# A hybrid layer on one core: S5 blocks in smaller TensorE tiles, a new order in both attentions, and the order of the last banks

## What is computed

```python
hn = rms_norm(h, norm_mix); proj = hn @ w_in          # u, q, k, v of 512 each
y_ssm = s5_mixer(u, ...)                              # 32 groups, 64 complex states each
y_att = moba_attention(q, k, v, rel_bias)             # 8 heads of 64, blocks of 256
mixed = concat([rms_norm(y_ssm, g1), rms_norm(y_att, g2)])
h = h + mixed @ w_out
h = h + memory_cross_attention(rms_norm(h, g3), rms_norm(mem, g4), x_wq, x_wkv, x_wo, x_qn, x_kn)
h = h + conv_ffn(rms_norm(h, g5), ffn_w_up, conv_w, conv_b, ffn_w_down)
```

## Time and profile before

| | |
|---|---|
| median of three runs | 713.04 us (709.05 to 714.66) |
| the profiled execution | 710.0 us |
| its span, first to last instruction | 708.4 us |
| PE busy | 694.4 us (98% of the span) |
| PEld busy | 576.2 us (81%) |
| VectorE, ScalarE, GpSimd busy | 412.8, 316.3, 142.6 us |
| granted TensorE clock | 1.000 of full |
| DMA | 73.94 MB, mean 104 GB/s |

### The profile page before, as it was taken

How to read it: one execution, slowest core, us unless ns; L and a number is a source line. 1 busy time by engine, 2 the same in 40 slices (tenths; PEclk the granted TensorE clock), 3 DMA queues, 4 the chain that set the end, 5 groups by cost and what they waited for, 6 DMA issues and landing times.

```text
span 708.4 us, 10868 instructions
## 1 busy us (share of the span) xinstructions
PE 694.4 (98%) x3913; PEld 576.2 (81%) x3913; DVE 412.8 (58%) x697; ACT 316.3 (45%) x535; POOL 142.6 (20%) x139
## 2 busy tenths in 40 slices
PE   7999999999999999989999999999999999999998
PEld 7978888886777888878998888888888887888886
DVE  4998967737665556556965555555555563333333
ACT  5737344467744635663554433343333432322220
POOL 4899985033031111240100000000000000000000
PEclk9999999999999999999999999999999999999999
DMA  8748443277310033030313323233133132231303
GB/s 249 222 116 142 138 117 108 67 218 247 139 60 2 29 121 119 1 119 1 120 60 120 104 73 118 75 103 118 60 118 108 69 118 98 80 118 67 111 1 118
DMA packets 62998, 73.94 MB, mean 104 GB/s; under 512 B 20873, under 2 KB 47796, under 8 KB 62836
## 3 DMA queue, kind: packets, MB, share of 16 engines
q1 hardware_dynamic: 59172, 66.12, 29.5%
q10 hardware_dynamic: 3792, 7.36, 3.3%
HBM read 68.08 MB, written 5.78 MB: 104 GB/s over the span
## 4 chain that ended last, share of the span: by engine, by line
PE 88%; POOL 4%; DVE 3%; ACT 2%; DMA 1%; issue 1%; SPq 0%; ACTq 0%; DVEq 0%; POOLq 0%
PE pb L514 25%; PE pb L516 25%; PE pb L515 25%; PE pb L1797 9%; PE pb L1800 4%; POOL F L692 2%; DMA raw<-in_w_in 1%; ACT F L900 1%; DVE F L1282 1%; ACT xs L900 0%; DVE wring L500 0%; ACT L900 0%; POOL F L805 0%; POOL F L808 0%; POOL rt L692 0%
## 5 line engine op out<-in xcount | busy, mean ns | idle before, releaser
L514 PE MATMUL pb<-xs,wring 128*128 128x512 f32 (+1 forms) x448 | 165.2, 369 | 1.2 <-POOL xs L832 0.7
L516 PE MATMUL pb<-xs,wring 128*128 128x512 f32 (+1 forms) x448 | 164.1, 366 | 0.0
L515 PE MATMUL pb<-xs,wring 128*128 128x512 f32 (+1 forms) x448 | 164.1, 366 | 0.0
L497 DVE TENSOR_TENSOR wring<-raw,wring 128x1024 fp32r<-128x1024 f32 x95 | 122.5, 1292 | 71.5 <-ACT wring L486 71.3
L486 ACT ACTIVATE wring<-raw 128x1024 fp32r<-128x1024 f32 x100 | 105.0, 1053 | 87.3 <-PE pb L516 75.0
L1288 DVE SCALAR_TENSOR_TENSOR F<-pb,ccol,F 128x511 f32<-128x511 f32 x88 | 66.0, 750 | 103.4 <-ACT F L900 97.5
L514 PE MATMUL pb<-wring,bs 128*128 128x512 f32 x240 | 96.1, 400 | 1.3 <-DVE bs L1288 0.9
L514 PEld LDWEIGHTS pb<-xs,wring 128*128 128x128 f32 x448 | 84.5, 189 | 15.7 <-POOL xs L832 1.2
L516 PEld LDWEIGHTS pb<-xs,wring 128*128 128x128 f32 x448 | 84.5, 189 | 13.7
L515 PEld LDWEIGHTS pb<-xs,wring 128*128 128x128 f32 x448 | 84.5, 189 | 13.5
L516 PE MATMUL pb<-wring,bs 128*128 128x512 f32 x240 | 93.6, 390 | 0.0
(11 more groups left out here) (147 smaller groups left out, 788.4 us busy)
## 6 DMA issues: line engine op xcount, KB each, us to landing
raw<-in_ffn_w_up SPq DMA_DIRECT2D x22, 1024.0 KB, 5.1
raw<-in_ffn_w_down SPq DMA_DIRECT2D x11, 1024.0 KB, 4.8
F<-in_x SPq DMA_DIRECT2D x8, 512.0 KB, 5.6
raw<-in_w_in ACTq DMA_DIRECT2D x4, 1024.0 KB, 5.6
raw<-in_w_out SPq DMA_DIRECT2D x4, 1024.0 KB, 5.0
raw<-in_w_in SPq DMA_DIRECT2D x3, 1024.0 KB, 6.0
raw<-in_x_wkv ACTq DMA_DIRECT2D x3, 1024.0 KB, 6.0
raw<-in_x_wq SPq DMA_DIRECT2D x2, 1024.0 KB, 6.2
```

Source lines behind the costliest of these rows:

```text
L497: ins = nc.vector.tensor_tensor(w_unit(u, 1), raw_unit(u), w_unit(u, 0).bitcast(f32), ALU.subtract)
L514: nc.tensor.matmul(ps, lh, rh, start=first, stop=False)
L515: nc.tensor.matmul(ps, lh, rl_, start=False, stop=False)
L516: return nc.tensor.matmul(ps, ll, rh, start=False, stop=last)
```

## The change

**S5 on TensorE.** In `kernels_in` the four pairs a go to four groups of 32 partitions of the bank and of array columns (before: to four column ranges of one bank at partition 0), and the loop over the parts is outside the loop over a. ScalarE copies each pair out by itself: eight operations of 16 by 128 in place of two of 16 by 512. In `outputs` each matmul is cut in two halves of 64 weight columns, c = 0 and 1, which go to the lower and upper 64 partitions of the same bank.

**Order around the own attention.** The write of the last quarter of S5's output is issued before chunk 12 (the gate's weight) is loaded; `skip_in(3)` and `gelu(3)` stand one step earlier, at 4; unit 26 is split at step 9 (before 8), unit 27 at 11 (before 9); the second tile of the memory's values is copied at 9 (before 8); the low part of unit 29 is taken at step 18 behind `ya_scale(1)` (before at 17, ahead of it).

**Memory attention.** One piece of the query projection less goes ahead of the loop, and each step from 0 to 15 has one piece: steps 0 to 6 the query projection, 7 to 15 the output projection. Transposes, high and low parts of the outputs are one step earlier, `qx_rows(2)` and `(3)`, their sums and roots one or two later, the residual of tile 0 is at 10 and 12, half of that of tile 1 at 14. All four low parts of `x_wo` on GpSimd stand ahead of the power of query tile 3 (before: two of the four). `QXT_BANK`, `XO_BANK` and `W_BANK` give other banks.

**Down projection.** The banks are taken in the order 4, 5, 6, 7, 0, 1, 2, 3, and the outputs leave in that order.

```diff
-XO_AT = [4, 5, 6, 8]
+XO_AT = [5, 6, 7, 8]
-SPLIT_AT = {0: 22, 1: 23, 2: 24, 4: 25, 8: 26, 9: 27, 13: 28, 16: 29, 29: 30, 31: 31}
+SPLIT_AT = {0: 22, 1: 23, 2: 24, 4: 25, 9: 26, 11: 27, 13: 28, 16: 29, 29: 30, 31: 31}
...
-        XO_BANK, W_BANK = (0, 2, 1, 7), (0, 1, 2, 0, 3, 1, 2, 3)
+        D_ORDER = (4, 5, 6, 7, 0, 1, 2, 3)
+        QXT_BANK, XO_BANK, W_BANK = (0, 1, 2, 0), (1, 0, 1, 7), (2, 1, 2, 0, 2, 1, 3, 2)
...
             load_chunk(sync, 11)
+            y_write(NQ - 1)
             load_chunk(sync, 12)
             y_back(NQ - 1)
...
                 if EV[i][0] == "qx2":
                     pool.wait_ge(lo_done, U_XO)
-                    output_low(0)
-                    output_low(1)
-                if EV[i][0] == "qx3":
-                    output_low(2)
-                    output_low(3)
+                    for n in range(4):
+                        output_low(n)
...
                 for b, n in enumerate("ab"):
-                    evac(f"k{n}{q}", kt[0:CG].rearrange("p (a b) n -> p a b n", b=2)[:, :, b, :],
-                         lambda p: p[0:CG, :].rearrange("p (a n) -> p a n", a=QP))
+                    p = read(act, f"k{n}{q}")
+                    for a in range(QP):
+                        last = A_(kt[0:CG, 2 * a + b, :], p[32 * a:32 * a + CG, 0:128], ACT.Copy)
+                    drained(last, f"k{n}{q}")
...
-                if s == 5:
+                if s == 4:
                     gelu(3)
-                if s in (7, 8):
-                    mem_rows("mv", xv, s - 7)
+                if s in (7, 9):
+                    mem_rows("mv", xv, s // 9)
...
-                if s - 1 in SPLIT_AT:
+                if s - 1 in SPLIT_AT and SPLIT_AT[s - 1] != U_OUT + 3:
                     split_lo(dve, SPLIT_AT[s - 1])
+                if s == 2 * H + 2:
+                    split_lo(dve, U_OUT + 3)
...
-                if s in (3, 7):
-                    qx_event(2 + s // 4)
-                if s in (2, 4, 8):
+                if s in (4, 8):
+                    qx_event(1 + s // 4)
+                if s in (2, 6, 10):
                     root(f"qx{1 + s // 4}", qr_ready)
...
-                for a in range(QP):
-                    at = slice(a * (L + 1) * CG, a * (L + 1) * CG + L * CG)
-                    for part in range(2):
+                for part in range(2):
+                    for a in range(QP):
+                        at = slice(a * (L + 1) * CG, a * (L + 1) * CG + L * CG)
                         for b in range(2):
                             rows = slice(b * NS, (b + 1) * NS)
-                            last = mm(p[b][0:CG, a * 128:(a + 1) * 128], bb[rows, part, q * QP + a, :],
+                            last = mm(p[b][32 * a:32 * a + CG, 0:128], bb[rows, part, q * QP + a, :],
                                       ca[rows, q % 2, part, at], part == 0, part == 1)
...
-                    mm(p[b][:, a * NC:(a + 1) * NC], toep[:, g, :], ub[:, q * QG + g, :], True, False)
-                at = slice((a * (L + 1) + 1) * CG, (a + 1) * (L + 1) * CG)
+                    for c in range(2):
+                        half = slice(c * 64, c * 64 + 64)
+                        mm(p[b][half, a * NC:(a + 1) * NC], toep[:, g, half], ub[:, q * QG + g, :], True, False)
+                at = (a * (L + 1) + 1) * CG
                 for part in range(2):
-                    for b in range(2):
-                        rows = slice(b * NS, (b + 1) * NS)
-                        last = mm(p[b][:, a * NC + 1:(a + 1) * NC], ca[rows, q % 2, part, at],
-                                  zb[rows, part, a, 0:NC - 1], False, part == 1)
+                    for c in range(2):
+                        half = slice(c * 64, c * 64 + 64)
+                        for b in range(2):
+                            rows = slice(b * NS, (b + 1) * NS)
+                            last = mm(p[b][half, a * NC + 1:(a + 1) * NC],
+                                      ca[rows, q % 2, part, at + c * 64:at + c * 64 + 64],
+                                      zb[rows, part, a, 0:NC - 1], False, part == 1)
...
-                if s < 2 * XH - 2:
-                    if s == 2:
+                if s < 2 * XH - 1:
+                    if s == 3:
                         x2_ready(3)
-                    xq_piece((s + 2) // XH + 2, (s + 2) % XH)
-                elif s >= 2 * XH:
-                    if s % XH == 0:
-                        after_drain(pe, f"xo{s // XH - 2}")
-                    xo_piece(s // XH - 2, s % XH)
+                    xq_piece((s + 1) // XH + 2, (s + 1) % XH)
+                else:
+                    if (s + 1) % XH == 0:
+                        after_drain(pe, f"xo{(s + 1) // XH - 2}")
+                    xo_piece((s + 1) // XH - 2, (s + 1) % XH)
...
-                for b in range(8):
+                for b in D_ORDER:
```

63 lines of the change are left out of this document (32 added, 31 removed).

## The result

| | before | after |
|---|---|---|
| median of the runs | 713.27 us (709.05 to 714.66) | 704.87 us (704.0 to 705.36) |
| profiled execution | 710.0 us, span 708.4 | 705.13 us, span 703.5 |

The ratio is 0.9917 (0.9888 to 0.9947). A second timing of the changed kernel on another chip gave 703.15 us against 709.73, 0.9903 (0.9888 to 0.9917). The medians are thus 6.6 to 8.4 us apart, the two profiled executions 4.9 us; 9.8 had been forecast for the latter. (The recorded ratio is not the quotient of the two medians, which is 0.988 in the first timing.)

A forecast was written before the change was run, and what follows sets the result against it. PE, busy 98% of the span, was taken as the bound. S5 6.3, own attention 2.0, memory attention 0.8 and down projection 0.7 summed to 9.8 us, from 710.0 to 700.2; median put at 702, forecast range 698 to 705.

The forecast's parts named there:

- rival (4): Tiles work, but early gelu(3) and late power cost what the other edits save: 703, median 705; chance 0.14.
- rival (2): S5's tiles pay in part: matmul starts become the limit, output pieces gain nothing; 704, median 706; chance 0.17.
- S5's tiles, the work: PE in S5: 0.20 us less for each of 16 output pieces, 1.2 less for each of four quarters' kernels.
- Rivals (1) to (3): S5's tiles: (1) only two at once, 0.12; (2) part of it, 0.17; (3) slower, column tiles exclude each other, 0.07.
- S5's tiles, the gain: S5 gives 6.3 us (0 to 7.5), with 1.5 arriving past VectorE's scan and 4.8 behind it.
- Behind it no such close meeting is left: S5 after VectorE's scan: savings of quarters 1 to 3 arrive in full, 4.8 us.
- The three other quarters have 2 us or more: S5's Toeplitz tables after the first quarter: 2 us or more of room before PE would wait for them.
- The own attention (a): Gate's first piece: earlier result write and gelu(3) shorten its wait for GpSimd; net 0.6 us gained, after 0.3 for probabilities.
- (b): Own attention step 8: PE's 1.13 us wait for ScalarE's copy of the probabilities shrinks, 0.7 gained.
- (c): Own attention step 18: PE's 0.90 us wait for `ya_scale(1)` shrinks as it goes ahead of unit 29's low part, 0.7 gained.
- Memory attention: Projection pieces cover PE's 1.8 us idle at steps 6 to 8; 0.8 gained (-0.3 to 1.8), VectorE setting the up projection's start.
- Down projection: First down unit's wait at bank 3 is covered by taking that bank last; 0.7 us gained.

The follow-up runs named there:

- S5 alone: Kernel before with S5's small array tiles (kernels_in, outputs, ScalarE's copies), all orders as before: median 708.56 against 709.70 us, ratio 0.9984, profiled 707.6.
- the orders as a whole: Changed kernel with S5's matmuls and copies as before, leaving the attention and down projection orders: median 706.45 against 709.70 us, ratio 0.9953.
- all in order: Changed kernel with reordered loads and splits, gelu(2) behind two probabilities, gelu(3) and skip_in(3) at step 5, chunk 12 before last write: 702.93 against 710.19 us, 0.9884.
- kernels' tiles alone: Kernel before with only the eight tiles for S5's kernels and ScalarE's eight copies: median 711.58 against 711.34 us, ratio 0.9996, profiled 707.7.
- gelu alone back: Changed kernel with gelu(3) and skip_in(3) back at step 5, last write still ahead of chunk 12: median 702.48 against 709.73 us, ratio 0.9907.
- second version of the bias: Changed kernel with chunk 10, then bias, ahead of quarter 2's read; gelu(0), gelu(1) and low parts earlier, gelu(2), skip_in(2) later: 704.58 against 711.34 us, 0.9883.

## Why the prediction was right in its time, and where its steps failed

The time, 704.87 against 702, is in the range, but that is partly luck. It lies at the upper edge of the forecast's 698 to 705 and nearest to rival (4), *the orders don't pay*, with 705; a median alone doesn't choose between them and rival (2) with 706. The sum behind it, 9.8 us, was twice what the traces show (4.9, of which 0.8 is start-up). Two steps failed, and a term is missing: the sum has nothing for the clock, which took 1.7 us in the profiled execution and up to 3.4 in others.

- **S5's tiles, the work**: right. Piece 1.09 us (forecast 1.07 to 1.17), kernels' block 0.58 (0.6), together 8.4 us of PE's work (3.2 + 4.8 = 8.0). Rivals (1) to (3) fall. The rule of the Trainium skill (TensorE: Matmul & The Clock Gate, Part 3) that a weight load overlaps a running matmul only where the row group differs would let column tiles gain nothing, as the prediction reads it; these rows disagree: the column tiles save the time in full.
- **S5's tiles, the gain**: wrong. The scan's wait was foreseen (over 1 us; 1.51 measured, though not in every execution). "Behind it no such close meeting is left" and "The three other quarters have 2 us or more" failed: I had looked for room at the next engine and not at the transfers. The last table had 2 us only as long as chunk 10's load came after it; with PE early, ScalarE issued that load before the table's last DMA. And behind it the loads, the bias and the first probabilities were a chain: in the seven traces with all tiles and the bias where it was, PE waits 1.5 to 2.9 us between 140 and 158, wherever the waits sit. S5 alone gave 1.1 us in the median and 2.4 in the profiled execution, not 6.3.
- **The own attention (a)**: wrong in sign. Forecast 0.6 gained; the gate's 0.73 went and 2.75 came. "units 24 and 25 are split later; they are needed at step 8 only" looked at PE's need, but ScalarE takes its steps in order, and its copies for step 5 stand behind the split. The early gelu(3) with its two table loads was priced at 0.3 and cost 0.99 even without S5. To that extent rival (4)'s mechanism came true, though the orders as a whole paid 3.3 us. The prediction named this among what would show it wrong: a wait for probabilities at step 6 of over 1 us; it was 1.73.
- **(b) and (c)**: right, 0.72 and 0.70 against 0.7 each.
- **Memory attention**: 0.9 against 0.8, with the up projection's start set by VectorE, now with a wait of 1.00 at it. No wait at bank 2. **Down projection**: 0.8 against 0.7.
- The rest is start-up and clock: PE was 0.8 us earlier at 43 us already, and the kernel before's median was 3.3 above its profiled execution in the first timing, 0.3 below it in the second, where all its executions had the full clock.

Not tried: all in order with gelu(3) at step 4. Open: what makes the clock fall in one execution and not in the next, on which the spread of the kernels' tiles alone (7.6 us) hangs.

## What to carry to other kernels

When an edit makes the busiest engine early, follow every queue at the place where it will arrive: an order between two queues that held by a microsecond is no order. A wait of an in-order engine is paid by what stands behind it there, whoever needs the awaited thing; and where removing one wait leaves the time as it was, look for where it came back. Compare when the next transfer's user starts in each trace, but ask in each what issued the transfer: equal times can have different causes, as chunk 12's had. And take the granted clock of each execution along: here it moved the time by as much as the edits did.

## What the runs showed of the hardware

- 24 records of an output piece, 8 on 128x64 tiles and 16 on 64x64, take 0.77 us; 32 records on eight tiles of 64 rows by 16 used columns take 0.58 us, against 1.85 on two tiles of 64 rows.
- DMAs issued just behind a 1 MB load can land after 6 us instead of 2.4, on another queue too: the load was on ScalarE's queue, the delayed ones (64 KB and 256 KB) on SyncE's. A 64 KB DMA issued 0.6 us ahead of the load landed after 2.4.
- After some waits of PE its granted clock fell to the lower level: after 2.12 us in the changed kernel (0.52 for 3.5 us), 2.12 with gelu alone back, 2.49 and 1.76 us, and after 1.53 and 1.51 us in S5's tiles alone. After 2.14 us in the second version of the bias it stayed at 1.00, as after 1.51 us at the scan and 1.73 us at step 6 in the changed kernel. So the length of the wait alone doesn't decide it; what does, these runs don't show. In one place it makes a wait cost nearly twice its length.
- The time of an execution goes with its mean granted clock: the same kernel took 707.7 us at 1.000 and 715.3 at 0.990, another 709.1 at 1.000 and 715.5 at 0.995.
